# A modulation vector in a fused three-block kernel: products with ones on TensorE, or one VectorE instruction a block

## The reference, cut to what matters

```python
def third_block(x, c, positions, w_ada, b_ada, ...):
    ada = c @ w_ada[l] + b_ada[l]                  # c: 1 x 1024, w_ada: 1024 x 3072
    shift, scale, gate = jnp.split(ada, 3, axis=-1)
    h = rms_norm(x, norm_w[l]) * (1.0 + scale[:, None, :]) + shift[:, None, :]
    ...
    x = x + gate[:, None, :] * (merged @ w_out[l])
```

## Time and profile before

| | us |
|---|---|
| median of 3 runs | 1967.65 |
| lowest and highest | 1965.8, 1970.3 |
| span of the profiled execution | 1961.2 |

### The profile page before, as it was taken

How to read it: one execution, slowest core, us unless ns; L and a number is a source line. 1 busy time by engine, 2 the same in 40 slices (tenths; PEclk the granted TensorE clock), 3 DMA queues, 4 the chain that set the end, 5 groups by cost and what they waited for, 6 DMA issues and landing times.

```text
span 1961.2 us, 20936 instructions
## 1 busy us (share of the span) xinstructions
PE 1610.4 (82%) x9098; PEld 966.8 (49%) x9098; DVE 604.4 (31%) x1395; ACT 294.3 (15%) x793; POOL 11.6 (1%) x35
## 2 busy tenths in 40 slices
PE   9999999999999999866556666555666566899999
PEld 7775567755688886322222222212222212457886
DVE  3673455634242412411201111101111101145533
ACT  1243313432112001100000000000000000223220
POOL 0000000000000000000000000000000000000000
PEclk9999999999999999987788887788887778999999
DMA  9761276423443463899999999999999999944200
GB/s 367 252 159 51 99 267 214 130 89 119 169 148 129 177 252 149 349 430 434 428 433 430 430 431 430 432 429 432 429 430 430 432 431 429 371 153 172 92 38 22
DMA packets 92869, 553.34 MB, mean 282 GB/s; under 512 B 4480, under 2 KB 11392, under 8 KB 79968
## 3 DMA queue, kind: packets, MB, share of 16 engines
q1 hardware_dynamic: 91920, 548.81, 69.9%
q0 software_dynamic: 848, 3.05, 0.4%
HBM read 550.80 MB, written 1.05 MB: 281 GB/s over the span
## 4 chain that ended last, share of the span: by engine, by line
PE 62%; DMA 34%; DVE 2%; ACT 1%; issue 0%; SPq 0%; POOL 0%; ACTq 0%; DVEq 0%; POOLq 0%
PE bank L664 29%; DMA ring<-in_w 21%; DMA arena<-in_w 12%; PE bank L1129 8%; PE bank L691 6%; PE bank L673 6%; PE bank L1157 3%; PE bank L652 3%; PE bank L1447 1%; PE bank L873 1%; PE bank L805 1%; PE bank L785 1%; DMA prm<-in_pk 0%; DVE arena L2098 0%; PE bank L1400 0%; PE bank L1100 0%
## 5 line engine op out<-in xcount | busy, mean ns | idle before, releaser
L664 PE MATMUL bank<-arena,ring 128*128 128x256 f32 x1856 | 412.2, 380 | 1.0 <-DVE arena L2356 0.5
L1129 PE MATMUL bank<-ring,arena 128*32 128x512 f32 x1216 | 288.0, 732 | 150.3 <-DMA arena<-in_w 98.6
L664 PEld LDWEIGHTS bank<-arena,ring 128*128 128x128 f32 x1856 | 348.9, 190 | 50.9 <-issue 4.3
L1129 PE MATMUL bank<-arena 128*32 128x512 f32 x832 | 234.8, 736 | 100.8 <-DMA ring<-in_w 100.8
L1129 PEld LDWEIGHTS bank<-ring,arena 128*32 128x32 f32 x1216 | 72.2, 132 | 272.3 <-issue 272.3
L664 PE MATMUL bank<-ring,arena 128*128 128x512 f32 (+3 forms) x520 | 205.1, 544 | 1.0 <-DVE arena L2468 1.0
L1129 PEld LDWEIGHTS bank<-arena 128*32 128x32 f32 x832 | 57.2, 132 | 187.4 <-issue 187.2
L1157 PE MATMUL bank<-ring,arena 128*32 128x512 f32 x576 | 118.8, 659 | 24.1 <-DMA arena<-in_w 13.4
L664 PEld LDWEIGHTS bank<-ring,arena 128*128 128x128 f32 x520 | 96.2, 190 | 83.4 <-issue 71.3
L691 PE MATMUL bank<-ring,arena 128*128 128x512 f32 (+1 forms) x320 | 127.4, 555 | 1.3 <-DVE arena L1970 0.5
L673 PE MATMUL bank<-arena,ring 128*64 128x256 f32 x1024 | 112.7, 380 | 0.0
(11 more groups left out here) (394 smaller groups left out, 1414.5 us busy)
## 6 DMA issues: line engine op xcount, KB each, us to landing
ring<-in_w SPq DMA_DIRECT2D x53, 4096.0 KB, 31.6
arena<-in_w SPq DMA_DIRECT2D x35, 4096.0 KB, 37.1
ring<-in_w_in SPq DMA_DIRECT2D x40, 2048.0 KB, 7.9
ring<-in_w_ada SPq DMA_DIRECT2D x6, 2048.0 KB, 13.5
ring<-in_w_out SPq DMA_DIRECT2D x6, 2048.0 KB, 8.2
arena<-in_w SPq DMA_DIRECT2D x6, 2048.0 KB, 11.9
ring<-in_w SPq DMA_DIRECT2D x6, 2048.0 KB, 8.4
ring<-in_w_out SPq DMA_DIRECT2D x16, 512.0 KB, 10.7
```

The source lines that it names most:

```text
L664: i = te.matmul(ps, lhsT, rhs, start=n0 + k == 0, stop=n0 + k == n - 1)
L1129: m = te.matmul(ps[32 * j:32 * j + 32, :], LM.xg[:, f, 128 * k + 32 * j:128 * k + 32 * j + 32], vs[j][:, 512 * (k % 2):512 * (k % 2) + 512 ...
```

## The change

The 3072x1024 weights are transposed on the host (`_modulation_rows`) into six blocks of 128 partitions x 4096: outputs are on the partitions, four outputs' rows of 1024 inputs behind each other. A row of `c` is loaded to all partitions by GpSimd (`ada_c`, 128x1024, at the place of earlier scratch), once in layer 0, and again in layer 1, since the state-space part writes over it; the second load waits for the end of layer 0 on three engines. VectorE's `modulation` now multiplies the 1024 inputs of an output by `c` and sums them with `accum_out` in the same instruction, straight into the column of `mod`: 24 instructions of 128x1024 in place of 48 of 128x512. They are taken one in each q step and one in every second za step in layer 0, and two or one in a q step in layer 1. Bias and scale follow at the end of layer 1's, in two instructions. TensorE's `modulation` is gone, with its six groups. The diff, without the changes to argument lists and the line that makes the semaphore:

```diff
@@ -434,7 +435,7 @@
 
         LN0 = dict(scale=prm[:, PK2 + 304:PK2 + 312], bias=prm[:, PK2 + 312:PK2 + 320])
 
-        ada = [ar(20800 + 512 * n, 512) for n in range(3)]
+        ada_out, ada_c = ar(20800, 1024), ar(21824, 1024)
 
         ADA = {(name, ly, g): 3 * ly + n for ly in range(2) for n, (name, g) in enumerate((("q", 1), ("za", 0), ("za", 1)))}
 
@@ -461,12 +462,11 @@
                 le.dma_start(h[:, tt, :], x[0, 128 * tt:128 * tt + 128]).then_inc(h_sem[tt], 16)
                 at.put(("h", -1, tt), h_sem[tt], 16)
             tokens(0)
-            wad = w_ada_3[0].rearrange("(c p) n -> p c n", p=128)
 
             def layer_load(name, *srcs, **kw):
                 if name in ADA:
                     n = ADA[name]
-                    load(("ada", n), (whole, wad[:, :, 512 * n:512 * n + 512]))
+                    load(("ada", n), (lambda v: v.rearrange("p c n -> p (c n)"), w_mod[n]), width=1024, kc=4)
                 load(name, *srcs, **kw)
             for ly in range(2):
                 wv = w_in[ly].rearrange("(c p) n -> p c n", p=128)
@@ -705,15 +705,6 @@
             def both(*name):
                 return [("ev", *name, j) for j in range(2)]
 
-            def modulation(n):
-
-                ps = fresh("mod", n)
-                t.wait_ge(*at.of("ada", n))
-                for k in range(4):
-                    i = te.matmul(ps[:, k:k + 1], ada[n % 3][:, 128 * k:128 * k + 128], ones[:, 0:1], start=True, stop=True)
-                i.then_inc(*t.done("mm", "mod", n))
-
-
             def layer_proj(ly):
                 every = both("hT", ly, 0) + both("hT", ly, 1)
                 if ly == 0:
@@ -823,8 +814,6 @@
                 for n in range(4):
                     yield from layer_values(ly, n)
                     if n < 2:
-                        for k in range(2 - n):
-                            modulation(3 * ly + 2 * n + k)
                         yield from layer_scores(ly, n + 2)
                 yield
 
@@ -2014,37 +2003,28 @@
                 behind()
                 ve.tensor_tensor(dst, dst, w1, ALU.mult).then_inc(*v.step())
 
-            def modulation(n):
-                c_n, c_b, k = PK3, PK3 + 16, 4 * n
-                v.wait_ge(*at.of("mm", "mod", n))
-                v.wait_ge(*at.of("prm", 1))
-                ps = bank("mod", n)
-                if n < 4:
-                    ve.tensor_tensor(mod[:, k:k + 4], ps[:, 0:4], prm[:, c_b + k:c_b + k + 4], ALU.add
-                                     ).then_inc(*v.done("ev", "mod", n))
-                else:
-                    ve.tensor_copy(mod[:, k + 8:k + 12], ps[:, 0:4]).then_inc(*v.done("ev", "mod", n))
-                if n == 5:
-                    ve.scalar_tensor_tensor(mod[:, 16:24], mod[:, 8:16], 1.0, prm[:, c_n:c_n + 8], ALU.add, ALU.mult
+            def modulation(ly):
+
+                ready(("ada_c", ly), ("prm", 1))
+                for n in range(3 * ly, 3 * ly + 3):
+                    w = weights(("ada", n), 1024, 4)
+                    v.wait_ge(*at.of("w", ("ada", n)))
+                    for k in range(4):
+                        o = 4 * n + k if n < 4 else 4 * n + 8 + k
+                        behind()
+                        ve.scalar_tensor_tensor(ada_out, w[:, k, :], 1.0, ada_c, ALU.mult, ALU.mult,
+                                                accum_out=mod[:, o:o + 1]).then_inc(*v.step())
+                        if k == 3:
+                            v.also("used", ("ada", n))
+                        if n < 5 or k < 3:
+                            yield
+                if ly:
+                    behind()
+                    ve.tensor_tensor(mod[:, 0:16], mod[:, 0:16], prm[:, PK3 + 16:PK3 + 32], ALU.add).then_inc(*v.step())
+                    behind()
+                    ve.scalar_tensor_tensor(mod[:, 16:24], mod[:, 8:16], 1.0, prm[:, PK3:PK3 + 8], ALU.add, ALU.mult
                                             ).then_inc(*v.done("mod"))
-
-            def modulation_sums(ly):
-
-                for n in range(3 * ly, 3 * ly + 3):
-                    to, w = ada[n % 3], weights(("ada", n))
-                    ready(("w", ("ada", n)), ("prm", 1))
-                    for c in range(8):
-                        cc = prm[:, PK3 + 8 + c:PK3 + 9 + c]
-                        if c == 0:
-                            ve.tensor_scalar(to, w[:, c, :], cc, None, ALU.mult).then_inc(*v.step())
-                        else:
-                            behind()
-                            ve.scalar_tensor_tensor(to, w[:, c, :], cc, to, ALU.mult, ALU.add).then_inc(*v.step())
-                        if c == 7:
-                            v.also("ada", n)
-                            v.also("used", ("ada", n))
-                        yield
-
+                yield
 
             def layer_proj(ly):
                 C_W, C_B, C_DT, C_A, C_D, C_N, C_S = L1.prms(ly)
@@ -2071,9 +2051,9 @@
                 if ly:
                     norm_gains(0, 1)
                 yield
-                sums = modulation_sums(ly)
+                sums = modulation(ly)
                 for i in range(8):
-                    for _ in range(3 if ly else 2):
+                    for _ in range(2 if ly and i % 2 == 0 else 1):
                         next(sums)
                     if i % 2:
                         v.wait_ge(*at.of("mm", "q", ly, i))
@@ -2082,7 +2062,7 @@
                     yield
                 for i in range(8):
                     gated(("za", ly, i), L1.zaT[:, i, :], 256)
-                    if ly == 0:
+                    if ly == 0 and i % 2 == 0:
                         next(sums)
                     yield
                 def conv_gated(ch):
@@ -3087,6 +3065,10 @@
                              fill=1.0e30, base=0, pattern=[[1, 256]], channel_multiplier=-1).then_inc(*p.done("dist"))
             ln = Slot(ln_sem)
             for ly in range(2):
+                if ly:
+                    ready(("layer", 0, "PE"), ("layer", 0, "DVE"), ("layer", 0, "ACT"))
+                ge.dma_start(ada_c, bcast(c_3[0], 1024)).then_inc(ada_c_sem, 16)
+                at.put(("ada_c", ly), ada_c_sem, 16 + 16 * ly)
                 ready(("mm", "k", ly, 0), *([("h", 0, 0), ("h", 0, 1)] if ly else []))
                 ge.dma_start(L1.lng, bcast(ln_g[ly], 1024)).then_inc(*ln.inc())
                 ge.dma_start(L1.lnb, bcast(ln_b[ly], 1024)).then_inc(*ln.inc())
@@ -3196,6 +3178,11 @@
     return np.concatenate([w[:, :, 1280:1536], w[:, :, 5120:5136]], axis=2)
 
 
+def _modulation_rows(i):
+
+    return i["w_ada_3"][0].T.reshape(6, 4, 128, 1024).transpose(0, 2, 1, 3).reshape(6, 128, 4096)
+
+
 def _by_partition(w):
 
     return w[0].reshape(64, 128, 4096).transpose(1, 0, 2)
```

More of the change, by code:

```diff
@@ L219, in program @@
             qn_rope_a_3, kn_nope_a_3, kn_rope_a_3, qn_b_3, kn_b_3, w_branch_a_3, w_branch_b_3, w_out_3,
-            rope_cs, w_vd, w2_last, pk1, pk2, pk_router, pk3, pos3, bgate3, out):
+            rope_cs, w_mod, w_vd, w2_last, pk1, pk2, pk_router, pk3, pos3, bgate3, out):
     ctx = ExitStack()
@@ L235, in program @@
         unit_sem = [sem(f"unit{i}_loaded") for i in range(10)]
+        ada_c_sem = sem("ada_c_loaded")
         h_sem = [sem(f"h{tt}_loaded") for tt in range(2)]
@@ L3240 @@
     pk3, pos3, bgate3 = _pack3(inputs, inv3)
-    given = [(n, _by_partition(inputs[n]) if n in ("w1_2", "w3_2", "w2_2") else inputs[n]) for n in _INS] + [("rope_cs", cs), ("w_vd", _v_dt(inputs)), ("w2_last", _last_by_columns(inputs)),
+    given = [(n, _by_partition(inputs[n]) if n in ("w1_2", "w3_2", "w2_2") else inputs[n]) for n in _INS] + [("rope_cs", cs), ("w_mod", _modulation_rows(inputs)), ("w_vd", _v_dt(inputs)), ("w2_last", _last_by_columns(inputs)),
                                                ("pk1", pk1), ("pk2", pk2), ("pk_router", pkr),
```

## The result

| | kernel before | changed kernel |
|---|---|---|
| median, 20 runs each | 1966.06 us | 1962.20 us |
| lowest, highest | 1964.54, 1970.30 | 1961.13, 1966.29 |
| span of the profiled execution | 1961.2 | 1960.1 |
| start of the experts' L1129 piece of the chain, now L1118 | 795.31 | 792.30 |

The ratio is 0.9981, 95% interval 0.9975 to 0.9988: 3.9 us less by the medians, forecast 3.2. The interval excludes 1, and it holds the forecast: 0.9975 to 0.9988 is 4.9 to 2.4 us. Timed again beside the experiments, the changed kernel has 1961.04 us against 1964.44, ratio 0.998 (0.9971 to 0.9989).

The account below looks back on a forecast made before the run. TensorE was taken to bound the layers; -5.72 (products) + 1.37 (c's broadcast) + 1.18 (banks) = -3.17 us took the 1967.65 us median to 1964.5 us, chance 0.50, range 1961.0 to 1969.0.

Parts of the forecast that it names:

- TensorE's products, -5.72: In both layers, removing TensorE's 48 modulation records takes 5.72 us off the chain of work.
- What is late next at 85 us: Layer 0's first scores: VectorE is just free when they come 1.88 us earlier, so all of it comes through.
- Rival C: VectorE, a block late at 84 us, holds up layer 0's scores; first gain shrinks by 1.4 us, 1965.9; chance 0.15.
- VectorE's part, 0: VectorE's 24 blocks in both layers, 1.41 us each, cost nothing on the path; cover 9.8 us in layer 1.
- Rival B, half rate: VectorE's accumulating multiply runs at half rate, 2.70 us a block; layer 1's scores wait 5.7 us, 1970.2; chance 0.12.
- The weights' layout, 0: Weight loads of 16 KB a partition in place of eight 2 KB rows, in the layers: worth nothing, either sign.
- c's broadcast, +1.37: At the start, c's 512 KB on full DMA delay the small parameter load and TensorE's second token half by 1.37 us.
- Banks, +1.18: Shifted bank rotation changes TensorE's waits at four places in layers and mixer: 0.88 + 0.30 - 0.78 + 0.78 us.
- The sum: Over the whole kernel, -5.72 + 1.37 + 1.18 = -3.17 us.
- Rival A: The costs of c's load at the start and of bank waits don't show: 1963.2 with half, 1961.2 with none; chance 0.23.
- From the layers to the end: After the layers, TensorE's progress releases the experts' loads, so an earlier layer end moves all behind by the same amount.
- The absolute number: Whole kernel: span 1958.0 us plus the 6.4 by which the median exceeded the profiled span gives 1964.5 us.

Follow-up runs that it names:

- the two kernels that differ in them: The kernel before with c's broadcast added, 1965.92 us, and the changed kernel with the bank counter stepped to the old places, 1960.03 us.
- the last experiment: The kernel before with only GpSimd's broadcast of c at the start added, into a tile nobody reads: 1965.92 us, ratio 1.0008.
- the experiment on it: The changed kernel with TensorE's bank counter stepped on where the removed products took banks, no products added: 1960.03 us, ratio 0.9980.
- the version without the costs: The changed kernel with c's broadcast held until the first parameters land and the bank counter stepped to avoid the four waits: 1958.05 us, ratio 0.9964.

## Why the prediction was right, point by point

**TensorE's products, -5.72.** Right: 5.71 by the kernel with unused products, less its slow group, and 5.69 by the two kernels that differ in them. What carried it is that I took them from the chain of work and not from their durations: 48 records of 250 ns overlap.

**What is late next at 85 us.** Right: nothing. Rival C ends in the row of 86.71, where VectorE still waits for TensorE. Even with each block twice there is no new wait of TensorE in layer 0.

**VectorE's part, 0.** Right. The block is 1.31 us for my 1.37 (1.41 with the gap). The slope of 1.05 ns a column was right and the base wrong: L1974 and the new form, which both take two operands from SBUF and the constant 1.0, are 682 and 1225 ns, 1.06 ns a column. I had started from L2042's 752 ns, a form that takes its scalar from `prm`; over 256 columns, too, the form with the scalar from `prm` takes 483 ns and one with a constant 419 (L2070). That the scalar makes these 64 to 70 ns is my reading; no run changes it alone. So the prediction's sentence that two operands from SBUF cost no more per column than one from PSUM was not carried by its numbers, 752 against 678; 682 against 678 carries it. The cover of 9.8 us in layer 1 was right too; the break-even is 2.19 for 2.23.

**Rival B, half rate.** Refuted by the 1225 ns, beside the 1220 ns of a multiply that sums nothing. The rule of the Trainium skill, Vector Engine (DVE) Microarchitecture Reference, section 7, that this instruction with two SBUF sources that aren't bf16 has half the throughput, since no port is left for the accumulator, doesn't hold here. Without an accumulator it doesn't either: 682 ns over 512 columns with both sources in SBUF, 678 with one in PSUM, and the form of 682 ns stands in the kernel before too. Had it held, a block would take 2.70 us; the doubled one takes 2.54, and that experiment is slower than the kernel before, ratio 1.0019.

**The weights' layout, 0.** Right: by the last experiment at the start, and from there to the experts by the 5.69 us above, in which it has a part of at most some hundredths.

**c's broadcast, +1.37.** The mechanism is right, the size a little low: 1.50 and 1.57 us in the two profiles of the changed kernel, 1.63 in the kernel before with c alone. Of the 1.50, 1.21 went when c was held back. From issue to landing the parameters take 1.33 us longer (10.34 for 9.01), near the 1.37 of c's 512 KB at 382 GB/s, and 0.1 to 0.2 us is their later issue on SyncE, which I hadn't counted.

**Banks, +1.18.** Right: the waits are 0.8 (for 0.88), 0.2 (for 0.30), -0.8 (for -0.78) and 0.8 (for 0.78), and the rotation as a whole is worth 1.21 us by the experiment on it, for 1.18. The waits alone add up to 1.0; the rest lies at the first place, where the group behind the wait of 0.8 us starts 0.98 us later (179.16 for 178.18). These came out of the order of groups and four rows of the kernel before, and none of them is in the diff.

**The sum.** -5.71 + 1.50 + 1.21 = -3.00, and the chain shows 792.30 - 795.31 = -3.01. Rival A, that the costs don't show, falls: both show in full.

**From the layers to the end.** "An earlier end of the layers moves the stream and all behind it by the same amount" fits the timed runs within their intervals, of +-1.3 us and more (-3.9 and -3.4 in the medians, and -2.99 for -3.0 in the version without the costs). One profile can't show it: the two things that vary by themselves, by 1.0 and 1.5 us, are each a third to a half of the effect.

**The absolute number.** 1964.5 was 2.3 us too high. It is the three runs' median, 1967.65, less 3.17: 1.6 of the 2.3 is that this median was high, where 20 runs give 1966.06, and 0.7 that the measured difference is 3.86, which the interval doesn't tell from 3.17. What I misread is the 6.4 us between the span and the median, which I took as what lies around the span. In the profiled executions whose own time is known, it is 1.7 to 1.8 us (1960.92 for a span of 1959.2, for one), and 2.0 in the kernel with doubled blocks. So of the 6.4 some 1.7 lies around the span, 1.6 is the high median, and 3.1 is that the profile was of an execution faster than the middle one. A difference taken from the profile survives that; a level does not.

## What to carry to other kernels

Moving small products off the bounding engine was worth their share of the chain of work here, to some hundredths of a microsecond once slow groups are accounted for, with measured cover on the other engine. Take their share from the chain and not from their durations; find the cover as a break-even duration per instruction, since it says how wrong one may be. Then look for what the move drags along and the diff doesn't show: a load that is issued at the start, where DMA is full and a 66 KB load is on the path, and a rotation of buffers that meets its fixed places elsewhere. Together they cost half of the gain here. Two lines that hold the load back gave 0.9972 and two more on the counter 0.9964, in place of 0.998; the chain tells these steps apart, the times only the whole.

## What the runs showed of the hardware that I hadn't expected

- Summing in the same instruction is nearly free: a multiply of two fp32 tiles from SBUF over 128x1024 takes 1225 ns with `accum_out` and 1220 without, and the read of the accumulator is an instruction of its own of 82 ns.
- A scalar_tensor_tensor that takes its scalar from a tile is longer than one with a constant, by 64 ns over 256 columns (483 for 419) and 70 over 512 (752 for 682). The forms differ in the order of their two operations too.
- A group of TensorE products takes 1.7 us more in some executions than in others, with nothing changed in it: the 16 of L691 at the start, 3.93 or 5.6 to 5.8 us (the changed kernel's first profile has 5.73 and its second 3.93), 16 of L664 at 330 us (5.34 for 3.65), the products behind the 4.17 us wait, and the last experts' 64 (8.53 to 10.08). Three of these lie where the granted clock has fallen. In the kernel with doubled blocks (the first two lines below, around the start and the 4.17 us wait) it falls behind idle time of 1.95 and 4.17 us; in the one with unused products (0.68 at 330 us, 0.50 from 331 to 333) TensorE had been busy without a gap for the 9.9 us before. But idle time of 1.9 to 2.0 us at the start is followed by no fall in four other profiles. For the slow start of the changed kernel's first profile and of the version without the costs (the last line below) the view shows 1.00, so that the clock is the cause there too is not shown. The last experts' 64 products follow a stage in which TensorE waits for loads, and the clock from 1667 to 1681 us is 0.58 to 0.90 in the nine profiles. What decides in which executions it happens stays open.

```profile
14.00:20.00 6.00, 5.72 (x18) 0.72 1.10 415
298.00:310.00 12.00, 7.83 (x70) 0.86 0.81 301
...
7.66:13.42 5.76, 5.76 (x18) 1.00 1.08 359
```

- Such a step puts chain starts of one kernel 1.7 us apart between executions, and it can hide a wait: in the first profile of the changed kernel TensorE seems to come to the second half just as its data is ready.
